# Turning the hidden activations of an FFN with TensorE through PSUM instead of VectorE blocks and block moves by DMA

## The chip, the cores and the metric

The kernel is one launch on one core of a Trainium2 chip. The metric is the device time of that launch in microseconds. Three runs of the kernel before are given, and one execution of it was recorded by the hardware profiler. Engines are called by the names of the profile: PE (TensorE matmuls), PEld (TensorE weight loads), DVE (VectorE), ACT (ScalarE), POOL (GpSimd) and SP (SyncE, which only issues loads here). A name with q behind it (SPq, POOLq) is the engine's queue that issues DMAs.

## What is computed

Two transformer blocks over x of 256 rows by 2048 columns, in float32. The first block has two layers, each with a mixer and a SwiGLU feed-forward; the second has two layers of mixers alone. What the change touches is the feed-forward of the first block:

```python
D_MODEL, SEQ, D_FF = 2048, 256, 5632
def _swiglu(u, w_gu, w_down):
    gate, up = jnp.split(u @ w_gu, 2, axis=-1)
    return (jax.nn.silu(gate) * up) @ w_down
```

u is the normed x. The result is normed again and added to x. Float32 accuracy is wanted from the whole.

## The kernel before

**Stages.** The kernel has six stages, numbered 0 to 5: mixer, FFN, mixer, FFN, mixer, mixer. Stages 1 and 3 are the two FFNs. Each stage multiplies by an input weight (the steps called col) and then by an output weight (the steps called row).

**Float32 by three products.** Each float32 operand is split into a high part (rounded to the fp32r type) and a low part (operand minus high part), and each product is made of three matmuls of 128x512: high times high, high times low, low times high (lines 1117 to 1119 in col, 1164 to 1166 in row). A weight slot is 128x1024 values, 512 KB, loaded by SP into one of four RAW buffers; ACT copies it to WH (line 1645), DVE subtracts to get WL (line 2184). Both are the step prep. A slot feeds 12 matmuls: 2 row tiles t of 128 rows, 2 halves j (or n), 3 products. There are three pairs WH, WL, and prep of slot s+3 can begin when the matmuls of slot s are done. In the order written out by hand, prep of a slot stands two slots ahead of its matmuls.

**An FFN stage.** The 11 chunks q of the 5632 hidden columns are 512 wide. For each q there is a col chunk of the gate (8 slots) and one of the up weight (8 slots). The results for t = 0 and t = 1 lie in two PSUM banks each, from banks 0 to 3. Step gate (ACT, line 1763) writes silu of the gate to the buffer G[q % 2][t] in SBUF, step mul (DVE, line 2267) multiplies it by the up result in place. So G[q % 2] holds a tile of 256 rows by 512 hidden columns with rows on the partitions. The output product needs hidden columns on the partitions, so the tile has to be turned. The row steps take the turned tiles HTH (high) and HTL (low), one k of 128 hidden columns at a time. All 44 k with the first half of the output columns come first (the function left), then 44 with the second half.

**How the tile is turned before.** Four steps, written into the order by the generator hidden, once per q (22 times in all):

- hx on DVE (line 2278): two instructions, each 128x512, that turn 32x32 blocks in place of their positions into the buffer TURNED.
- hx on POOL (line 2870): 16 DMAs of 32 KB each that move the blocks from their partitions to the right ones, into MOVED, which is the same memory as G.
- ht on ACT (line 1769): one copy of 128x1024 to HTH.
- hl on DVE (line 2284): one subtraction of 128x1024 to HTL.

In the order, hx of q stands behind the first slot of the next chunk, and ht and hl stand eight and nine slots later. The row step of k waits for hl of k // 4. The gate of q waits for hl of q - 2.

**PSUM and the order.** The banks 4 to 7 are a ring for short-lived results during the columns of a stage. Nothing of stages 1 and 3 uses it between the start of the columns and the second half of the rows. At the end of the stage before, the step uth (PE line 1092) makes groups of four 128x128 float32 transposes of x into such a bank with ident, the identity matrix in MK, as the other operand. In stage 0, the steps cv_tap (line 1208), cv_out (line 1218) and ot (line 1186 in stages 0, 2, 4 and 5) make the same kind of groups between the weight matmuls. Each engine runs its own instructions in the order of the one list; waits are on semaphores.

Of the kernel before, what the change touches and what calls it, by code (L numbers as in the profile page):

```python
# [121 lines left out]
class Banks:  # L122
# [10 lines left out]
    def take(self, pool, *name):  # L133
        b = min(pool, key=lambda i: self.turn[i])
        self.stamp += 1
        self.turn[b] = self.stamp
        self.before[name], self.now[b], self.where[name] = self.now[b], name, b
        return self.aps[b]
# [70 lines left out]
class Order:  # L209
# [6 lines left out]
    def put(self, *step):  # L216
        self.steps.append(step)
        self.done[step] = self.slot
# [22 lines left out]
def pause(n):  # L241
    for _ in range(n):
        yield
# [7 lines left out]
def write_order(slots):  # L251
# [182 lines left out]
    def ffn(st):  # L434
        def sink(c, t):
            if c % 2 == 0:
                put("gate", st, c, t)
            else:
                put("mul", st, c, t)

        def main():
            yield from cols(st, sink)
            yield from left(st)

        def hidden():
            for q in range(11):
                yield from need(("mul", st, 2 * q + 1, 1))
                yield
                put("hx", st, q)
                yield from pause(8)  # L450
                put("ht", st, q)
                yield
                put("hl", st, q)

        put("gb", st)
        together(main(), hidden())
        right(st)
        cross(st)
# [324 lines left out]
def build(nc, A, out):  # L783
    with ExitStack() as ctx:
# [9 lines left out]
        def steps(name, line=None, by=1):  # L794
            all_steps.append(Steps(ctx.enter_context(nc.semaphore(name)), line or Line(), by))
            return all_steps[-1]
# [10 lines left out]
        GB = WORK[:, 8704:10752]  # L807
        room = [work_at + 4096 * i for i in range(8)] + [big_at + 4 * a for a in (5184, 6400, 7424, 15360)]
        WHL += [(over(f"XH{i}", SLOT, room[2 * i]), over(f"XL{i}", SLOT, room[2 * i + 1])) for i in range(NX)]
        wc_at = -(-nc.sbuf_base // 32) * 32  # L810
        WC = sb("WC", 9 * 128, F32R)[:]
        MK = sb("MK", 8 * 128)[:]
        ONE = sb("ONE", 128)[:]
# [24 lines left out]
        HTL = [over("HTL0", 8192, work_at).rearrange("p (k n) -> p k n", k=32),  # L838
               over("HTL1", 3072, big_at + 4 * 11264).rearrange("p (k n) -> p k n", k=12)]
        G = [[BIG[:, 14336 + 1024 * x + 512 * t:14336 + 1024 * x + 512 * t + 512] for t in range(2)] for x in range(2)]  # L840
        G5 = [[g.rearrange("p (k b n) -> p b k n", k=4, b=4) for g in G[x]] for x in range(2)]
        TURNED = nc.alloc_sbuf_tensor_at("TURNED", [128, 1024], dtype=F32, offset=wc_at)[:]
        MOVED = [BIG[:, a:a + 1024] for a in (14336, 15360)]

        def by_blocks(x):
            return x.rearrange("p k (a n) -> p a k n", n=32)

        Z = v3(BIG, 2)
        ZR = v3(over("ZR", 2 * CHUNKS_EVEN, big_at), 2)
# [159 lines left out]
        def slot_of(s):  # L1009
# [3 lines left out]
            if wd < 64:  # L1013
# [2 lines left out]
            return (v3(x[:, 0:n], kk) for x in (RAW[s % NRAW], wh, wl))  # L1016

        pe, act, dve, pool = Line(), Line(), Line(), Line()
        p_mm, p_ut, p_gd, p_cv, p_hg, p_ns, p_b2 = (
            steps("s_pe_" + n, pe) for n in ("weights", "operand", "gdn", "conv", "hgrn", "nsa", "block2"))  # L1020
        a_hi, a_ut, a_ff, a_z, a_nm, a_gd, a_cv, a_hg, a_og, a_ns, a_b2 = (
            steps("s_act_" + n, act) for n in ("weights", "operand", "ffn", "sink", "norm", "gdn", "conv", "hgrn",
                                               "gate", "nsa", "block2"))
# [4 lines left out]
            steps("s_pool_" + n, pool) for n in ("norm", "nsa", "block2", "root"))  # L1028
        d_raw = [steps(f"s_dma_raw{i}", by=16) for i in range(NRAW)]
        d_x = [steps(f"s_dma_x{i}", by=16) for i in range(4)]  # L1030
        d_first, d_gain, d_const, d_gb, d_ntab, d_w1, d_tab2, d_turn, d_out = (
            steps("s_dma_" + n, by=16) for n in ("first", "norms", "const", "gain", "nsa_tables", "w1", "tables2",
                                                 "turned", "out"))

        def room_of(s):

# [21 lines left out]
        def tensor(e):  # L1058
# [88 lines left out]
            @step  # L1147
            def row(st, k, hf, s, ts, ns):
                raw, wh, wl = slot_of(s)
                xh, xl = (HTH[:, k], HTL[k // 32][:, k % 32]) if st in (1, 3) else (UTH[:, k], UTL[:, k])  # L1150
                on.wait_ge(*v_lo.of(s))
                if st in (1, 3):
                    on.wait_ge(*v_ff.of("hl", st, k // 4))
                else:
                    on.wait_ge(*v_ut.of("ot", st, k if st > 2 else k - k % 2))
                for t in ts:
                    for n in ns:
                        if k == (0 if hf else LEFT[st][0]):
                            banks.take([row_bank(st, t, 2 * hf + n)], "row", st, t, 2 * hf + n)
                            on.wait_ge(*banks.free("row", st, t, 2 * hf + n))  # L1160
                        o = banks.ap("row", st, t, 2 * hf + n)
                        cs = slice(512 * n, 512 * n + 512)
                        lh, ll = xh[:, 128 * t:128 * t + 128], xl[:, 128 * t:128 * t + 128]
                        e.matmul(o, lh, wh[:, 0, cs], start=k == (0 if hf else LEFT[st][0]), stop=False)  # L1164
                        e.matmul(o, lh, wl[:, 0, cs], start=False, stop=False)  # L1165
                        x = e.matmul(o, ll, wh[:, 0, cs], start=False, stop=k == (KTILES[st] - 1 if hf else LEFT[st][-1]))  # L1166
                x.then_inc(*(p_mm.inc("t0", s) if 1 not in ts else p_mm.inc("n0", s) if 1 not in ns else p_mm.inc(s)))

            @step
            def ot(st, k):  # L1170
                b = take("ot", st, k)
                for t in range(2):
                    if st == 0:
                        on.wait_ge(*v_og.of("o", k // 8, k % 8 // 4, t))
                    elif st == 2:
                        on.wait_ge(*v_ns.of("pv", k // 4, t, 2))
                    elif st == 4:
                        on.wait_ge(*v_b2.of("y", st, k // 2, t))
                    else:
                        on.wait_ge(*(v_b2.of("st_o", 3) if k else v_b2.of("yg")))  # L1180
                for j in range(2):
                    if st > 2:
                        b = b if j == 0 else take("ot", st, k + 1)
                    for t in range(2):
                        c = 128 * t if st > 2 else 256 * j + 128 * t
                        x = e.transpose(b[:, c:c + 128], operand_of(st, k + j, t), ident)
                    if j or st > 2:
                        x.then_inc(*p_ut.inc("ot", st, k + j if st > 2 else k))

            @step  # L1190
            def gates1():
# [438 lines left out]
        def scalar(e):  # L1630
# [125 lines left out]
            @step  # L1756
            def gate(st, c, t):
                q = c // 2
                on.wait_ge(*p_mm.of(col_end[st, c]))
                on.wait_ge(*g_rs.of("r", "pre", st))  # L1760
                if q >= 2:
                    on.wait_ge(*v_ff.of("hl", st, q - 2))
                e.activation(G[q % 2][t], banks.ap("acc", st, c, t), ACTF.Silu,
                             scale=HR[:, t:t + 1]).then_inc(*banks.empty(a_ff, "acc", st, c, t))

            @step
            def ht(st, q):
                on.wait_ge(*d_turn.of(st, q, 15))
                e.activation(by_blocks(HTH[:, 4 * q:4 * q + 4]), MOVED[q % 2].rearrange("p (a k n) -> p a k n", a=8, k=4),
                             ACTF.Copy).then_inc(*a_ff.inc("ht", st, q))  # L1770

            @step
            def stat(st, t, part):
# [399 lines left out]
        def vector(e):  # L2173
# [95 lines left out]
                v_ff.also("mul", st, q, t)  # L2269

            @step
            def hx(st, q):
                out = TURNED.rearrange("p (t b k n) -> p t b k n", t=2, b=4, k=4)
                if q or st == 3:
                    on.wait_ge(*d_turn.of(*((st, q - 1) if q else (1, 10)), 15))
                for t in range(2):
                    on.wait_ge(*v_ff.of("mul", st, q, t))
                    e.transpose(out[:, t], G5[q % 2][t]).then_inc(*v_ff.inc("hx", st, q, t))  # L2278

            @step  # L2280
            def hl(st, q):
                on.wait_ge(*a_ff.of("ht", st, q))
                hi, lo = HTH[:, 4 * q:4 * q + 4], HTL[q // 8][:, 4 * q % 32:4 * q % 32 + 4]
                e.tensor_tensor(by_blocks(lo), MOVED[q % 2].rearrange("p (a k n) -> p a k n", a=8, k=4),
                                by_blocks(hi.bitcast(F32)), ALU.subtract).then_inc(*v_ff.inc("hl", st, q))

            @step
            def root(st, t):
# [494 lines left out]
        def gpsimd(e):  # L2783
# [76 lines left out]
                                    ALU.add).then_inc(*g_ns.inc("blk", part, j))  # L2860

            @step
            def hx(st, q):
                src = TURNED.rearrange("p (t b n) -> p t b n", t=2, b=4)
                dst = MOVED[q % 2].rearrange("p (t a n) -> p t a n", t=2, a=4)
                for t in range(2):
                    on.wait_ge(*v_ff.of("hx", st, q, t))
                for a in range(4):
                    for b in range(4):
                        e.dma_start(dst[32 * b:32 * b + 32, :, a], src[32 * a:32 * a + 32, :, b]).then_inc(  # L2870
                            *d_turn.inc(st, q, 4 * a + b))

            @step
            def tables_2():
                stream_made(4)
                for dst, name in ((RT, "c_r32"), (RT16, "c_r16"), (LC, "c_lc"), (CA, "c_ca"), (LTT, "c_lt")):
# [121 lines left out]
```

## Time and profile before

| | |
|---|---|
| median of 3 runs | 2771.85 us (2770.7 to 2773.2) |
| profiled execution, its own time | 2770.7 us |
| its span, first to last instruction | 2768.9 us |
| PE busy | 2741.7 us (99%) |
| DVE busy | 1588.5 us (57%) |
| ACT busy | 1376.8 us (50%) |
| POOL busy | 248.8 us (9%) |
| moved by DMA | 492.67 MB, mean 178 GB/s |

The profiled execution took 1.8 us more than its span and 1.15 us less than the median. A busy time says how long an engine had an instruction in it, not that it could not have been fed faster: matmuls overlap, each is shown with its whole passage through the engine, and their ends are modelled. So for PE the distance from one start to the next is what counts.

### The profile page before, as it was taken

Reading aid. Unit: us, or ns where it says so; the run is one execution under the profiler, and the core shown is the slowest. Engines: PE = TensorE matmul, PEld = TensorE weight load, DVE = VectorE, ACT = ScalarE, POOL = GpSimd, SP = SyncE. Lnnn points to the kernel's source line nnn. Section 1 sums busy time; section 2 is a strip of 40 time slices with the busy share of each in tenths; the row PEclk is TensorE's granted clock in tenths of the full one; section 3 lists DMA queues with packets and bytes.
Section 4 is the critical chain, followed back from the end, with each engine's and each line's share of the span. In section 5 each row is a group of like instructions: output and inputs, shape, how many; then the busy total and the mean of one; then the engine's idle time right before and its main releaser. Section 6 shows DMA issues by size and latency. Waiting matters only on the chain.

```text
span 2768.9 us, 33142 instructions
## 1 busy us (share of the span) xinstructions
PE 2741.7 (99%) x13296; PEld 2284.7 (83%) x13296; DVE 1588.5 (57%) x2214; ACT 1376.8 (50%) x2033; POOL 248.8 (9%) x437
## 2 busy tenths in 40 slices
PE   9999999999999999999999999999999999999998
PEld 7788888888888888888788888888888888887877
DVE  5665777665555555444645555655555554466666
ACT  6655465555444444434644554644444443355565
POOL 0000000001122121100100000021212210000002
PEclk9999999999999999999999999999999999999999
DMA  7865544766677676665665434676767765564444
GB/s 237 136 134 136 108 110 103 175 207 190 201 209 207 203 208 202 201 194 191 213 185 148 137 107 152 192 211 201 209 200 209 207 204 193 195 207 162 160 140 134
DMA packets 224762, 492.67 MB, mean 178 GB/s; under 512 B 21216, under 2 KB 21984, under 8 KB 223968
## 3 DMA queue, kind: packets, MB, share of 16 engines
q1 hardware_dynamic: 210848, 467.78, 58.3%
q0 software_dynamic: 13616, 22.72, 2.4%
q8 instruction: 104, 1.70, 0.3%
q14 instruction: 50, 0.41, 0.0%
q10 hardware_dynamic: 144, 0.05, 0.0%
HBM read 476.84 MB, written 2.10 MB: 173 GB/s over the span
## 4 chain that ended last, share of the span: by engine, by line
PE 89%; DVE 5%; ACT 3%; DMA 1%; issue 1%; POOL 0%; SPq 0%; ACTq 0%; POOLq 0%
PE PS L1117 19%; PE PS L1119 19%; PE PS L1118 19%; PE PS L1164 8%; PE PS L1166 8%; PE PS L1165 8%; DVE WL L2184 2%; DVE WORK L2351 1%; ACT WH L1645 1%; PE PS L1375 1%; PE PS L1503 1%; PE PS L1272 1%; PE PS L1291 1%; PE PS L1092 1%; DVE XL L2184 1%
## 5 line engine op out<-in xcount | busy, mean ns | idle before, releaser
L2184 DVE TENSOR_TENSOR WL<-RAW,WH 128x1024 fp32r<-128x1024 f32 x826 | 1011.1, 1225 | 963.3 <-ACT WH L1645 957.4
L1645 ACT ACTIVATE WH<-RAW 128x1024 fp32r<-128x1024 f32 x830 | 875.4, 1056 | 869.7 <-PE PS L1119 558.5
L1117 PE MATMUL PS<-WH,UTH 128*128 128x512 f32 x2396 | 952.4, 397 | 7.3 <-DVE WL L2184 6.0
L1119 PE MATMUL PS<-WH,UTL 128*128 128x512 f32 x2396 | 935.0, 390 | 0.0
L1118 PE MATMUL PS<-WL,UTH 128*128 128x512 f32 x2396 | 934.2, 390 | 0.0
L1117 PEld LDWEIGHTS PS<-WH,UTH 128*128 128x128 f32 x2396 | 450.4, 188 | 104.7 <-DVE WL L2184 7.0
L1119 PEld LDWEIGHTS PS<-WH,UTL 128*128 128x128 f32 x2396 | 450.1, 188 | 96.5
L1118 PEld LDWEIGHTS PS<-WL,UTH 128*128 128x128 f32 x2396 | 450.7, 188 | 88.1
L1164 PE MATMUL PS<-WH,HTH 128*128 128x512 f32 x656 | 255.2, 389 | 0.0
L1165 PE MATMUL PS<-WL,HTH 128*128 128x512 f32 x656 | 255.2, 389 | 0.0
L1166 PE MATMUL PS<-WH,HTL 128*128 128x512 f32 x656 | 255.2, 389 | 0.0
L2870 POOL DMA_DIRECT2D BIG<-TURNED x352 | 186.1, 538 | 749.5 <-DVE TURNED L2278 672.1
L2792 POOL TENSOR_TENSOR SM<-SM 128x1 f32<-128x1 f32 (+2 forms) x25 | 27.5, 1098 | 1379.0 <-DVE SM L2188 1379.0
L1165 PEld LDWEIGHTS PS<-WL,HTH 128*128 128x128 f32 x656 | 123.1, 188 | 25.7
L1164 PEld LDWEIGHTS PS<-WH,HTH 128*128 128x128 f32 x656 | 123.1, 188 | 25.6
L1166 PEld LDWEIGHTS PS<-WH,HTL 128*128 128x128 f32 x656 | 123.1, 188 | 25.5
L1164 PE MATMUL PS<-WH,UTH 128*128 128x512 f32 x256 | 102.2, 399 | 1.4 <-DVE UTL L2232 1.4
L1166 PE MATMUL PS<-WH,UTL 128*128 128x512 f32 x256 | 99.9, 390 | 0.0
L1165 PE MATMUL PS<-WL,UTH 128*128 128x512 f32 x256 | 99.7, 390 | 0.0
L2184 DVE TENSOR_TENSOR XL<-RAW,XH 128x1024 fp32r<-128x1024 f32 x53 | 63.9, 1220 | 13.1 <-ACT XH L1645 13.0
L1676 ACT ACTIVATE UTH<-PS,GP 128x128 fp32r<-128x128 f32 x160 | 46.1, 386 | 39.7 <-PE PS L1092 39.7
L1645 ACT ACTIVATE XH<-RAW 128x1024 fp32r<-128x1024 f32 x53 | 55.2, 1066 | 19.2 <-DMA RAW<-in_ffn_w_down 7.7
(427 smaller groups left out, 2350.5 us busy)
## 6 DMA issues: line engine op xcount, KB each, us to landing
RAW<-in_ffn_w_gu SPq DMA_DIRECT2D x352, 512.0 KB, 4.5
RAW<-in_ffn_w_down SPq DMA_DIRECT2D x176, 512.0 KB, 4.6
RAW<-in_ab_w_in SPq DMA_DIRECT2D x128, 512.0 KB, 4.7
RAW<-in_nsa_w_in SPq DMA_DIRECT2D x80, 512.0 KB, 3.6
RAW<-in_w_in SPq DMA_DIRECT2D x64, 512.0 KB, 4.1
RAW<-in_ab_w_out SPq DMA_DIRECT2D x32, 512.0 KB, 3.6
RAW<-in_nsa_w_out SPq DMA_DIRECT2D x32, 512.0 KB, 3.9
BIG<-TURNED POOLq DMA_DIRECT2D x352, 32.0 KB, 3.4
```

What stands on the lines that cost most here:

```text
L1092: x = e.transpose(b[:, 128 * j:128 * j + 128], H[:, t, 128 * (4 * q + j):128 * (4 * q + j) + 128], ident)
L1117: e.matmul(o, lh, wh[:, j], start=k + j == 0, stop=False)
L1118: e.matmul(o, lh, wl[:, j], start=False, stop=False)
L1119: x = e.matmul(o, ll, wh[:, j], start=False, stop=k + j == NKT - 1)
L1164: e.matmul(o, lh, wh[:, 0, cs], start=k == (0 if hf else LEFT[st][0]), stop=False)
L1165: e.matmul(o, lh, wl[:, 0, cs], start=False, stop=False)
L1166: x = e.matmul(o, ll, wh[:, 0, cs], start=False, stop=k == (KTILES[st] - 1 if hf else LEFT[st][-1]))
L1272: x = e.matmul(b[:, 128 * h:128 * h + 128], LT[:, h], XX[:, h, 0], start=True, stop=True)
L1645: e.activation(wh, raw, ACTF.Copy).then_inc(*a_hi.inc(s))
L1676: e.activation(UTH[:, kk, 128 * t:128 * t + 128], b[:, 128 * j:128 * j + 128], ACTF.Copy, scale=GP[:, st, kk:kk + 1]).then_inc(*a_ut.inc(" ...
L2184: e.tensor_tensor(wl, raw, wh.bitcast(F32), ALU.subtract).then_inc(*v_lo.inc(s))
L2870: e.dma_start(dst[32 * b:32 * b + 32, :, a], src[32 * a:32 * a + 32, :, b]).then_inc(*d_turn.inc(st, q, 4 * a + b))
```

## The change

The turn is done by TensorE. For each q and each t a new PE step ht makes four 128x128 transposes of G[q % 2][t] into one bank of the ring 4 to 7. ACT copies that bank (128x512) to HTH, DVE subtracts to get HTL. The DVE block turns, the 16 DMAs of POOL and the buffers TURNED and MOVED are gone. In the order, ht of t = 0 stands behind the first slot of the next chunk and ht of t = 1 behind the second; for the last q both stand behind the first slot of the rows. The row step waits for the low part of t = 1, the gate of q for the transposes of q - 2.

```diff
@@ order, ffn(st).hidden @@
             for q in range(11):
                 yield from need(("mul", st, 2 * q + 1, 1))
                 yield
-                put("hx", st, q)
-                yield from pause(8)
-                put("ht", st, q)
-                yield
-                put("hl", st, q)
+                for t in range(2):
+                    put("ht", st, q, t)
+                    if q < 10:
+                        yield
@@ tensor, row @@
-                    on.wait_ge(*v_ff.of("hl", st, k // 4))
+                    on.wait_ge(*v_ff.of("ht", st, k // 4, 1))
@@ tensor @@
+            def ht(st, q, t):
+                g = G[q % 2][t]
+                b = take("ht", st, q, t)
+                on.wait_ge(*v_ff.of("mul", st, q, t))
+                for j in range(4):
+                    x = e.transpose(b[:, 128 * j:128 * j + 128], g[:, 128 * j:128 * j + 128], ident)
+                x.then_inc(*p_ht.inc(st, q, t))
@@ scalar, gate @@
-                    on.wait_ge(*v_ff.of("hl", st, q - 2))
+                    on.wait_ge(*p_ht.of(st, q - 2, t))
@@ scalar @@
-            def ht(st, q):
-                on.wait_ge(*d_turn.of(st, q, 15))
-                e.activation(by_blocks(HTH[:, 4 * q:4 * q + 4]), MOVED[q % 2].rearrange("p (a k n) -> p a k n", a=8, k=4),
-                             ACTF.Copy).then_inc(*a_ff.inc("ht", st, q))
+            def ht(st, q, t):
+                on.wait_ge(*p_ht.of(st, q, t))
+                e.activation(HTH[:, 4 * q:4 * q + 4, 128 * t:128 * t + 128], v3(banks.ap("ht", st, q, t), 4),
+                             ACTF.Copy).then_inc(*a_ff.inc("ht", st, q, t))
@@ vector @@
-            def hx(st, q):
-                ...
-            def hl(st, q):
-                ...
+            def ht(st, q, t):
+                lo = HTL[q // 8][:, 4 * q % 32:4 * q % 32 + 4, 128 * t:128 * t + 128]
+                on.wait_ge(*a_ff.of("ht", st, q, t))
+                e.tensor_tensor(lo, v3(banks.ap("ht", st, q, t), 4),
+                                HTH[:, 4 * q:4 * q + 4, 128 * t:128 * t + 128].bitcast(F32),
+                                ALU.subtract).then_inc(*banks.empty(v_ff, "ht", st, q, t))
@@ gpsimd @@
-            def hx(st, q):
-                ...
-                for a in range(4):
-                    for b in range(4):
-                        e.dma_start(dst[32 * b:32 * b + 32, :, a], src[32 * a:32 * a + 32, :, b]).then_inc(
-                            *d_turn.inc(st, q, 4 * a + b))
```

## Rows read from the trace of the kernel before

**Rows 1.** The page, shares of the engines and 40 slices

```profile
PE 2741.7 (99%) x13296; PEld 2284.7 (83%) x13296; DVE 1588.5 (57%) x2214; ACT 1376.8 (50%) x2033; POOL 248.8 (9%) x437
PEclk9999999999999999999999999999999999999999
```

**Rows 2.** Busy time by stretch: the two FFN stages, then one with four transpose groups

```profile
640.00:1320.00 680.00, 680.00 (x3003) 562.99 (x3003) 350.31 (x318) 293.66 (x307) 93.80 (x178) 1.00 0.67 202
1790.00:2468.00 678.00, 678.00 (x2993) 561.41 (x2992) 349.76 (x311) 291.21 (x293) 94.81 (x178) 1.00 0.67 203
...
616.00:624.00 8.00, 8.00 (x44) 6.64 (x43) 7.15 (x15) 5.99 (x16) 0.00 (x0) 1.00 0.62 175
```

**Rows 3.** Instructions of single lines: ns shortest/median/longest, first and last start

```profile
L2278 DVE STREAM_TRANSPOSE TURNED<-BIG x44: 669/688/707, 671.8 to 2249.4; 128x512 f32<-128x512 f32 x44
L2870 POOL DMA_DIRECT2D BIG<-TURNED x352: 533/539/575, 673.8 to 2258.7; - x176
L1769 ACT ACTIVATE HTH<-BIG x22: 1043/1057/1057, 693.2 to 2269.1; 128x1024 fp32r<-128x1024 f32 x22
L2284 DVE TENSOR_TENSOR HTL<-BIG,HTH x22: 1216/1218/1221, 696.4 to 2273.1; 128x1024 fp32r<-128x1024 f32 x22
L1688 ACT ACTIVATE UTH<-PS x8: 592/596/610, 1646.2 to 1705.4; 128x512 fp32r<-128x512 f32 x8
L2242 DVE TENSOR_TENSOR UTL<-PS,UTH x8: 680/686/692, 1646.8 to 1706.1; 128x512 fp32r<-128x512 f32 x8
L1092 PE MATMUL PS<-MK,H x160: 270/272/273, 617.4 to 2641.4; 128*128 128x128 f32 x160
```

**Rows 4.** Timeline of PE: start us, us, line; two transpose groups twelve matmuls apart

```profile
53.20 0.39 PE L1119 MATMUL PS<-WH,UTL 128*128 128x512 f32 x1
53.44 0.60 PE L1218 MATMUL PS<-MK,WORK 128*128 128x128 f32 x4
53.79 0.49 PE L1117 MATMUL PS<-WH,UTH 128*128 128x512 f32 x1
54.11 0.39 PE L1118 MATMUL PS<-WL,UTH 128*128 128x512 f32 x1
54.34 0.39 PE L1119 MATMUL PS<-WH,UTL 128*128 128x512 f32 x1
...
56.42 0.39 PE L1119 MATMUL PS<-WH,UTL 128*128 128x512 f32 x1
56.66 0.60 PE L1218 MATMUL PS<-MK,WORK 128*128 128x128 f32 x4
```

**Rows 5.** Timeline of PE, stage 1: 36 starts during DMAs of POOL, 57 without

```profile
673.91 0.39 PE L1117 MATMUL PS<-WH,UTH 128*128 128x512 f32 x1
...
682.07 0.39 PE L1117 MATMUL PS<-WH,UTH 128*128 128x512 f32 x1
...
1090.75 0.39 PE L1117 MATMUL PS<-WH,UTH 128*128 128x512 f32 x1
...
1103.67 0.39 PE L1117 MATMUL PS<-WH,UTH 128*128 128x512 f32 x1
```

**Rows 6.** Timeline of DVE, ACT, PE and POOL around the end of the first chunk pair

```profile
668.92 0.39 PE L1119 MATMUL PS<-WH,UTL 128*128 128x512 f32 x1
669.35 1.41 DVE L2267 SCALAR_TENSOR_TENSOR BIG<-PS,SM,BIG 128x512 f32<-128x512 f32 x2 [0.34 <-PE PS L1119]
670.68 1.22 DVE L2184 TENSOR_TENSOR WL<-RAW,WH 128x1024 fp32r<-128x1024 f32 x1
671.87 0.39 PE L1117 MATMUL PS<-WH,UTH 128*128 128x512 f32 x1
672.13 1.06 ACT L1645 ACTIVATE WH<-RAW 128x1024 fp32r<-128x1024 f32 x1 [1.66 <-PE PS L1119]
673.23 1.23 DVE L2184 TENSOR_TENSOR WL<-RAW,WH 128x1024 fp32r<-128x1024 f32 x1
673.80 8.47 POOL L2870 DMA_DIRECT2D BIG<-TURNED  x16 [24.27 <-DVE TURNED L2278]
```

**Rows 7.** Timeline of PE, stage 5: a group whose result the next matmul needs

```profile
2602.53 0.39 PE L1166 MATMUL PS<-WH,UTL 128*128 128x512 f32 x1
2602.76 0.60 PE L1186 MATMUL PS<-MK,BIG 128*128 128x128 f32 x4
2604.07 0.50 PE L1164 MATMUL PS<-WH,UTH 128*128 128x512 f32 x1 [0.71 <-DVE UTL L2232]
...
2604.64 0.39 PE L1166 MATMUL PS<-WH,UTL 128*128 128x512 f32 x1
```

More of the change, by code:

```diff
@@ L809, in build @@
         WHL += [(over(f"XH{i}", SLOT, room[2 * i]), over(f"XL{i}", SLOT, room[2 * i + 1])) for i in range(NX)]
-        wc_at = -(-nc.sbuf_base // 32) * 32
         WC = sb("WC", 9 * 128, F32R)[:]
@@ L840, in build @@
         G = [[BIG[:, 14336 + 1024 * x + 512 * t:14336 + 1024 * x + 512 * t + 512] for t in range(2)] for x in range(2)]
[L841 to L846, printed above, removed]
         Z = v3(BIG, 2)
@@ L1018, in build @@
         pe, act, dve, pool = Line(), Line(), Line(), Line()
-        p_mm, p_ut, p_gd, p_cv, p_hg, p_ns, p_b2 = (
-            steps("s_pe_" + n, pe) for n in ("weights", "operand", "gdn", "conv", "hgrn", "nsa", "block2"))
+        p_mm, p_ut, p_ht, p_gd, p_cv, p_hg, p_ns, p_b2 = (
+            steps("s_pe_" + n, pe) for n in ("weights", "operand", "hidden", "gdn", "conv", "hgrn", "nsa", "block2"))
         a_hi, a_ut, a_ff, a_z, a_nm, a_gd, a_cv, a_hg, a_og, a_ns, a_b2 = (
@@ L1030, in build @@
         d_x = [steps(f"s_dma_x{i}", by=16) for i in range(4)]
-        d_first, d_gain, d_const, d_gb, d_ntab, d_w1, d_tab2, d_turn, d_out = (
-            steps("s_dma_" + n, by=16) for n in ("first", "norms", "const", "gain", "nsa_tables", "w1", "tables2",
-                                                 "turned", "out"))
+        d_first, d_gain, d_const, d_gb, d_ntab, d_w1, d_tab2, d_out = (
+            steps("s_dma_" + n, by=16) for n in ("first", "norms", "const", "gain", "nsa_tables", "w1", "tables2", "out"))
         def room_of(s):
@@ L1188, in ot @@
                         x.then_inc(*p_ut.inc("ot", st, k + j if st > 2 else k))
+            @step
+            def ht(st, q, t):
[5 more added lines that the diff above has]
+                x.then_inc(*p_ht.inc(st, q, t))
             @step
@@ L2271, in hx @@
             @step
-            def hx(st, q):
[L2273 to L2280, printed above, removed]
-            def hl(st, q):
[L2282 to L2285, printed above, removed]
+            def ht(st, q, t):
[4 more added lines that the diff above has]
+                                ALU.subtract).then_inc(*banks.empty(v_ff, "ht", st, q, t))
             @step
@@ L2862, in hx @@
             @step
-            def hx(st, q):
[L2864 to L2867, printed above, removed]
-                for a in range(4):
-                    for b in range(4):
-                        e.dma_start(dst[32 * b:32 * b + 32, :, a], src[32 * a:32 * a + 32, :, b]).then_inc(
-                            *d_turn.inc(st, q, 4 * a + b))
-            @step
             def tables_2():
```

## The prediction

> **What bounds the kernel now.** I read the page first. PE is busy 99% of the span and its granted clock stands in the top tenth in all 40 slices; DVE has 57%, ACT 50%, POOL 9% [rows 1]. That is an average, so I asked for the two FFN stages alone. From 640 to 1320 us PE is busy 680.00 of 680.00 us, from 1790 to 2468 us 678.00 of 678.00, both at clock 1.00 (the 2.4 GHz level), while DVE and ACT work about half of either stretch [rows 2]. The reader is to see that in the stages the change touches PE never sits idle. But a matmul is shown with 0.39 us although the next one starts sooner, so "busy" would hide slack in the feeding. The timeline decides: 36 starts from 673.91 to 682.07 us are 8.16 us, or 0.2267 us each; 57 starts from 1090.75 to 1103.67 are 12.92 us, again 0.2267 [rows 5]. PE runs the stages in lockstep, one 128x512 matmul every 0.2267 us, and nothing else shows in this rhythm. So a thing taken from DVE, ACT, POOL or the DMA queues brings nothing there, and a thing put into PE's queue costs its full distance between starts, once for each time it is done. As the instructions of PE are strictly one behind another through all six stages, what is lost in stages 1 and 3 is not won back later.
>
> **What is removed.** Per q: two block turns on DVE, 2 x 0.688 = 1.38 us; the subtraction, 1.22 us; the copy on ACT, 1.06 us; 16 DMAs issued by POOL, 16 x 0.539 = 8.6 us of POOL [rows 3]. Over 22 q that is 57 us of DVE, 23 of ACT and 190 of POOL. I count all of it as 0 us of time: it lies beside PE's matmuls, and PE waits for none of it in the stretches of [rows 2]. The moves are 352 x 32 KB = 11.5 MB; a lighter load on the DMA engines could only help if PE waited for weights, and it doesn't there.
>
> **What is added off PE.** Per q two copies of 128x512 out of PSUM on ACT and two such subtractions on DVE. The same forms stand in stage 2: 0.596 and 0.686 us [rows 3]. So ACT has 1.19 us per q in place of 1.06, DVE 1.37 in place of 2.60. Cost 0 us, hidden behind the twelve matmuls of a slot (12 x 0.2267 = 2.72 us), if prep of the weights stays in time. Behind the waiting copy on ACT stands prep of slot s+4, and PE waits for that. Take s as the last slot of a chunk pair, with its last matmul at 668.92 [rows 6]. Today prep of s+3 ends on DVE at 670.68 + 1.22 = 671.90, and slot s+3 begins at 669.15 + 2 x 2.72 = 674.59 (669.15 is 668.92 + 0.23): 2.7 us in hand. After the change the group of t = 0 comes behind slot s+1, at 671.87. Its four transposes end near 672.47, the copy ends near 673.2, prep of s+4 on ACT near 674.3, on DVE near 675.5. Slot s+4 begins at 674.59 + 2.72 plus about 1.0 for the two groups, 678.3. Again about 2.8 us in hand: the lateness of prep and the lateness of its user nearly cancel. If that cover were gone, the copies and subtractions would stand in PE's way, at most 44 x (0.596 + 0.686) = 56 us.
>
> **The new wait on PE.** Each group waits for its mul. In [rows 6] the two mul run from 669.35 to 670.76, the first ends near 670.1, and PE gets to its group at 671.87: 1.7 us early; the second group, a slot later, has 4 us. For the last q both groups stand 2.72 us behind the last column matmul, with the second mul done after about 1.8 (668.92 to 670.76): 0.9 us in hand. The bank of the ring was emptied long before, since nothing else uses banks 4 to 7 here. The gate's wait falls earlier than before, not later. The low part of a chunk is needed by rows that are far behind, even for the last q (its first k is the 41st row slot). Cost 0.
>
> **What is added on PE.** 2 stages x 11 q x 2 t = 44 groups of four, 176 transposes, all in the queue that sets the end. The same thing (four 128x128 float32 transposes between fp32r matmuls of 128x512, wait fulfilled) stands in the trace many times. In [rows 4], from the matmul before the group at 53.20 to the third behind it at 54.34 are 1.14 us, of which three matmul distances are 0.68: 0.46 us. That isn't all: the matmuls behind a group start 0.23 us apart, not 0.2267, for a while. From 53.20 to 56.42 there are twelve matmuls and one group: 3.22 - 2.72 = 0.50 us. At other such places the twelve-matmul reading gives 0.48 to 0.51, so I take 0.50, since ten of eleven pairs of groups here stand just twelve matmuls apart, as those of [rows 4]. The two groups of the last q stand side by side; the second then costs only the 0.45 of its own distance. Sum: 40 x 0.50 + 2 x 0.95 = 21.9 us. Bounds: 44 x 0.45 = 19.8 and 44 x 0.51 = 22.4.
>
> **Sum.** Against the profiled execution: span 2768.9 + 21.9 = 2790.8, with the 1.8 us around it 2792.6. The median lies 1.15 above that execution, so the median after comes to 2771.85 + 21.9 = 2793.7 us, 0.8% slower. What a measurement of this kernel can tell from no change is about 0.2%, 5.5 us; the sum is four times that.
>
> **A price that reads otherwise.** The row of the transposes gives 272 ns for one [rows 3], and someone who goes by it gets 176 x 0.272 = 47.9 us, or 2820. I don't take it: four in a row are shown as 0.60 us, so (0.60 - 0.272) / 3 = 0.11 us lies between two starts [rows 4]; 272 ns is the passage of one through the array, which the neighbours overlap. The Trainium skill (TensorE: Matmul & The Clock Gate, "Part 4: PE-mode transpose") states about 275 ns for a transpose in a kernel's context and 390 ns alone. By that rule the trace agrees on the duration, and taken as a cost it would give an estimate near 2820 us.
>
> **The rivals.**
>
> 1. *Each transpose costs its shown duration.* 2820 us. For it: nothing but the row of 272 ns. Against it: no group of the trace with its wait fulfilled costs over 0.51 us. Chance 0.03.
> 2. *A group waits, or makes prep late.* Its place is the first group of each q (mul not done) or slot s+4 (weights not ready). The margins are 1.7 us, 0.9 us in the last q, and 2.8 us, and it decides from there on. A group whose result the next matmul needs costs 2.11 - 0.68 = 1.43 us [rows 7], which is 0.93 more than a plain one; if all 44 were so, 2793.7 + 41 = 2835 us, if only the first of each q, 2814. A fall of the granted clock belongs here: four groups within 8 us leave it at 1.00 [rows 2], so I give that almost nothing. Chance of the whole rival 0.05.
> 3. *The transposes slip in free.* Then the time stays within 5.5 us of 2771.85, and a group must cost under 0.125 us. For it: weight loads overlap matmuls. Against it: none read costs under 0.45. It holds also the case that about 16 us come back from something I don't see. Chance 0.03.
> 4. *The moves slow the matmuls today, and their end pays for more than the transposes.* This is the one with the other sign: the FFN stages have 2 x (22 x 8 + 88) x 12 = 6336 matmuls; to get 5.5 us below 2771.85 they must gain 27.4 us, 4.3 ns of 226.7 each, giving 2766 us. Against it: the distance is 0.2267 us during the DMAs of POOL and without them [rows 5]. Chance 0.02. The Trainium skill (VectorE: DVE Perf Modes, "Rules for kernel authors") says to transpose 128x128 on TensorE where PSUM will do as the destination; as a rule for the time it would put the result on this side, and these rows don't bear it out in a kernel that PE bounds.
>
> **How the numbers follow.** The forecast has 0.87; all of it is slower by over 0.2%, with rivals 1 and 2 that makes 0.95 for slower, 0.03 for the same, 0.02 for faster. The bounds of the group's price give 2791.7 to 2794.3; the three runs lie 1.2 below and 1.4 above their median. With a little room for a few exposed waits the range is 2790 to 2797; it leaves out about 2 in 10, the rivals and the rim of the forecast.
>
> **What would show each step.** Right: in the page after, a new PE group of 128x128 with PS<-MK,BIG x176 at a line of its own; stages 1 and 3 each about 11 us longer, PE busy throughout; 3.22 us from the matmul before a group to the twelfth behind it; POOL down by about 190 us; DVE busy down by about 27 us and ACT up by about 3; no idle time ahead of the new group, and prep done over 2 us before its slot. Wrong: PE idle before the new group with DVE's mul as releaser, or before line-1117 matmuls with DVE's WL; a matmul distance other than 0.2267 us far from the groups; a clock under 1.00 in either stage.

## The result, and the profile after

The changed kernel takes 2792.58 us (median of 4 runs, 2790.19 to 2793.2). The kernel before, in the runs beside it, takes 2772.52. The ratio is 1.007 with a 95% interval of 1.0058 to 1.0083: 20.1 us slower. The profiled execution of the changed kernel has a span of 2790.9 us, 22.0 over the span of before.

The page after, its shares of the engines (compare [rows 1]):

```profile
PE 2763.0 (99%) x13472; PEld 2302.3 (82%) x13472; DVE 1566.4 (56%) x2192; ACT 1379.0 (49%) x2055; POOL 62.9 (2%) x85
```

PE has 176 instructions more, POOL has lost 186 us and DVE 22. The 186 us of POOL and the moves are gone from the profile, and the time went the other way.

The two FFN stages after, busy time by stretch (columns as in [rows 2]: stretch, its length, busy time and number of instructions of PE, PEld, DVE, ACT and POOL, granted clock, DMA share, GB/s):

```profile
640.00:1320.00 680.00, 680.00 (x3045) 562.74 (x3044) 331.68 (x299) 289.96 (x311) 1.23 (x2) 1.00 0.59 190
1801.00:2479.00 678.00, 678.00 (x3033) 561.15 (x3032) 331.17 (x293) 286.64 (x296) 1.23 (x2) 1.00 0.60 192
```

PE is as full as before and the clock stays at 1.00. What changed is what PE is full of. The timeline of PE after, stage 1, from the last matmul of a chunk pair over both groups of its q (answers to [rows 4]):

```profile
670.40 0.39 PE L1110 MATMUL PS<-WH,UTL 128*128 128x512 f32 x1
...
673.12 0.40 PE L1110 MATMUL PS<-WH,UTL 128*128 128x512 f32 x1
673.36 0.60 PE L1187 MATMUL PS<-MK,BIG 128*128 128x128 f32 x4
673.71 0.49 PE L1108 MATMUL PS<-WH,UTH 128*128 128x512 f32 x1
674.03 0.39 PE L1109 MATMUL PS<-WL,UTH 128*128 128x512 f32 x1
674.27 0.39 PE L1110 MATMUL PS<-WH,UTL 128*128 128x512 f32 x1
...
676.35 0.39 PE L1110 MATMUL PS<-WH,UTL 128*128 128x512 f32 x1
676.58 0.60 PE L1187 MATMUL PS<-MK,BIG 128*128 128x128 f32 x4
...
1115.07 0.39 PE L1108 MATMUL PS<-WH,UTH 128*128 128x512 f32 x1
...
1118.24 0.39 PE L1157 MATMUL PS<-WH,HTL 128*128 128x512 f32 x1
1118.47 1.03 PE L1187 MATMUL PS<-MK,BIG 128*128 128x128 f32 x8
1119.26 0.48 PE L1155 MATMUL PS<-WH,HTH 128*128 128x512 f32 x1
...
1136.81 0.39 PE L1157 MATMUL PS<-WH,HTL 128*128 128x512 f32 x1
```

From 673.12 to 676.35 there are twelve matmuls and one group: 3.23 - 2.72 = 0.51 us. To see what all groups cost, follow one and the same matmul through both traces. The last of the first chunk pair starts at 668.92 before [rows 6] and at 670.40 after, 1.48 later, ahead of any group. The one at 1103.67 before [rows 5] starts at 1115.07 after, 11.40 later. Between them lie 20 groups: 9.92 / 20 = 0.496 us each. The timeline of PE before has the partner of the last line:

```profile
1124.52 0.39 PE L1166 MATMUL PS<-WH,HTL 128*128 128x512 f32 x1
```

There the lag is 12.29: the eight transposes of the last q, side by side, cost 0.89. So stage 1 loses 9.92 + 0.89 = 10.81 us, and stage 3, read in the same way, again 10.81. That is 21.6 of the 22.0 us of span.

The new instructions by line, after (columns as in [rows 3]; under the groups stands who waits):

```profile
L1187 PE MATMUL PS<-MK,BIG x176: 270/272/273, 673.4 to 2270.9; 128*128 128x128 f32 x176
L1769 ACT ACTIVATE HTH<-PS x44: 595/599/600, 674.0 to 2271.2; 128x512 fp32r<-128x512 f32 x44
L2275 DVE TENSOR_TENSOR HTL<-PS,HTH x44: 678/691/694, 674.6 to 2272.0; 128x512 fp32r<-128x512 f32 x44
```

No line under the first of them names anything that PE waited for. The copy and the subtraction take 599 and 691 ns, as their likes in [rows 3].

### The profile page after: what moved, and what is told of

It reads as the page before. It is cut to its first block, busy times and chain, and to the rows that moved or that the text cites. A ratio compares the mean times of both kernels' runs of the same rounds, so it can differ in the third digit from the quotient of the medians.

```text
span 2790.9 us, 33039 instructions
## 1 busy us (share of the span) xinstructions
PE 2763.0 (99%) x13472; PEld 2302.3 (82%) x13472; DVE 1566.4 (56%) x2192; ACT 1379.0 (49%) x2055; POOL 62.9 (2%) x85
## 4 chain that ended last, share of the span: by engine, by line
PE 89%; DVE 5%; ACT 3%; DMA 2%; issue 1%; POOL 0%; SPq 0%; ACTq 0%; POOLq 0%
PE PS L1108 19%; PE PS L1110 19%; PE PS L1109 19%; PE PS L1155 8%; PE PS L1157 8%; PE PS L1156 8%; DVE WL L2184 2%; DVE WORK L2343 1%; ACT WH L1645 1%; PE PS L1375 1%; PE PS L1503 1%; PE PS L1272 1%; PE PS L1187 1%; PE PS L1291 1%; PE PS L1083 1%
## 5 line engine op out<-in xcount | busy, mean ns | idle before, releaser
L1769 ACT ACTIVATE HTH<-PS 128x512 fp32r<-128x512 f32 x44 | 26.1, 599 | 78.2 <-PE PS L1187 78.2
```

## The experiments

Seven kernels ran, in two sets, each beside runs of the kernel before. In the first set, with a median of 2771.03 us for before, ran the changed kernel once more, the groups beside the old path, both groups side by side, and one by one. In the second, with 2770.6, ran the change without its transposes, twice the groups, and the groups ahead of their data. The lag of a kernel is read as above, as the start of one and the same matmul in its trace minus that in the trace of before.

**The changed kernel once more.**

> The changed kernel as it is, once more, beside the runs below. Theory (44 groups of four transposes in PE's queue, each 0.49 to 0.50 us, the last pair 0.89, nothing else): 21.6 us above before, so near 2793, span about 2791. Rival (the difference is mostly chance between executions of a program): the difference to before would wander by several us from the first measurement's 20.1.

2792.9 us (5 runs, 2791.67 to 2793.23), span 2791.1, ratio 1.0076 (1.0064 to 1.0089). The lag over stage 1 is again 10.81 us and over stage 3 again 10.81. The difference isn't chance.

**Groups beside the old path.** The kernel before with transposes of x that nobody reads:

```diff
                 put("hx", st, q)
-                yield from pause(8)
+                put("hd", st, q, 0)
+                if q < 10:
+                    yield
+                put("hd", st, q, 1)
+                yield from pause(7 if q < 10 else 8)
@@ tensor @@
+            def hd(st, q, t):
+                b = take("hd", st, q, t)
+                for j in range(4):
+                    e.transpose(b[:, 128 * j:128 * j + 128], H[:, t, 128 * j:128 * j + 128], ident)
```

> The kernel before with all of its DVE turns, POOL moves, copies and subtractions, and beside them 44 groups of four 128x128 float32 transposes of x into unused banks, at the places in PE's queue where the change puts its own; nobody reads them. Theory (what the change takes from DVE, POOL and the DMA queues is worth nothing, the groups are all): 21.6 us over before, the time of the changed kernel, near 2793. Rival (the moves cost something today, which the change saves, and the transposes cost that much more than shown): above the changed kernel by that saving, 2795 to 2800.

2793.59 us (4 runs, 2790.76 to 2794.48), ratio 1.0078 (1.0063 to 1.0094), span 2791.4. Its page:

```profile
PE 2763.2 (99%) x13472; PEld 2302.6 (82%) x13472; DVE 1588.5 (57%) x2214; ACT 1376.7 (49%) x2033; POOL 249.3 (9%) x437
```

DVE, ACT and POOL work as much as in [rows 1], PE as much as after the change, and the time is that of the change. By the lag, stages 1 and 3 lose 10.75 us each, against 10.81 after the change. The 186 us of POOL, the 22 us of DVE and 11.5 MB of moves that the change saves are worth nothing that can be measured.

**The change without its transposes.** ACT and DVE read the unturned tile in SBUF (the copy waits for mul in place of the transposes, and the output product is left wrong); the cut shows the copy, and the subtraction is edited likewise:

```diff
-                for j in range(4):
-                    x = e.transpose(b[:, 128 * j:128 * j + 128], g[:, 128 * j:128 * j + 128], ident)
...
-                e.activation(HTH[:, 4 * q:4 * q + 4, 128 * t:128 * t + 128], v3(banks.ap("ht", st, q, t), 4),
+                e.activation(HTH[:, 4 * q:4 * q + 4, 128 * t:128 * t + 128], v3(G[q % 2][t], 4),
```

> The changed kernel without the transposes: ACT copies and DVE subtracts straight from the unturned tile in SBUF, in the same places, so the hidden activations are left unturned and the output product is of the wrong layout; all else is as in the changed kernel. Theory (PE's queue is all): the time of before, 2772 to 2773, although DVE, POOL and DMA are relieved. Rival (the relief is worth something and the transposes cost more than 21.6 us): below before by over 2 us, 2765 to 2770. Rival (the added copies and subtractions cost something): above before, 2775 or more.

2770.93 us (10 runs, 2769.65 to 2772.99) against 2770.6, ratio 1.0 (0.9991 to 1.0009), span 2769.2. Its page:

```profile
PE 2743.0 (99%) x13296; PEld 2286.3 (83%) x13296; DVE 1562.9 (56%) x2192; ACT 1381.1 (50%) x2055; POOL 63.2 (2%) x85
```

Here the relief of POOL and DVE is there and the transposes are not, and the time is that of before. The lag moves by 0.02 us at most over either FFN stage. The two kernels close the question from both sides: the transposes alone are the 21 us.

**Twice the groups.** The changed kernel and, four slots after its own groups, two of x into unused banks (hd as above):

```diff
+                if q == 10:
+                    yield
+                yield from pause(2)
+                for t in range(2):
+                    put("hd", st, q, t)
+                    yield
```

> The changed kernel with 44 more groups of four transposes, of x, into unused banks, at the fifth and sixth slots of the chunk after, each twelve matmuls or more from any other group. Theory (each group adds 0.49 to 0.50 us of PE's queue): 21.8 us above the changed kernel, near 2814. Rival (part of the first 44 was a one-off price such as a wait or a code effect, not a price per group): the second 44 add clearly less or more than the first, under 19 or over 25 us.

2812.76 us (4 runs, 2812.34 to 2814.11), ratio 1.0151 (1.0136 to 1.0166), span 2811.1. That is 19.9 over the changed kernel run in the other set and 20.0 by the spans, short of the 21.8 expected and not far above the 19 at which the rival begins. The lags decide against that rival: over stage 1 the kernel loses 21.78 us, over stage 3 21.79, so 43.6 in all and 22.0 for the second 44 groups (none of which stand side by side). The missing 2 us lie outside the FFN stages, where executions of one kernel differ too (last section).

**Both groups of a q side by side.**

```diff
                 yield
-                for t in range(2):
-                    put("ht", st, q, t)
-                    if q < 10:
-                        yield
+                put("ht", st, q, 0)
+                put("ht", st, q, 1)
```

> Both groups of a q stand side by side behind the first slot of the next chunk, as in the last q, so PE makes eight transposes in a row; 22 pairs in all. Theory (a transpose costs 0.11 us, and each return from transposes to fp32r matmuls costs about 0.05 us more, once per return): a pair costs 0.89 instead of 0.99 us, 20 x 0.10 = 2.0 us less than the changed kernel, near 2790.6, span about 2789. Rival (the cost is per transpose alone, 0.124 each however they stand): no difference, 2792.6. Second rival (the second bank of a pair waits for the second mul): slower than the changed kernel, with PE idle ahead of the transposes.

2789.97 us (5 runs, 2787.59 to 2791.81), span 2787.9. That is 2.9 us less than the changed kernel beside it by the medians, but the runs of the two touch. The timeline of PE is what decides:

```profile
671.76 0.40 PE L1108 MATMUL PS<-WH,UTL 128*128 128x512 f32 x1
672.00 1.04 PE L1185 MATMUL PS<-MK,BIG 128*128 128x128 f32 x8
672.79 0.48 PE L1106 MATMUL PS<-WH,UTH 128*128 128x512 f32 x1
673.11 0.40 PE L1107 MATMUL PS<-WL,UTH 128*128 128x512 f32 x1
673.34 0.39 PE L1108 MATMUL PS<-WH,UTL 128*128 128x512 f32 x1
673.57 0.39 PE L1106 MATMUL PS<-WH,UTH 128*128 128x512 f32 x1
673.80 0.39 PE L1107 MATMUL PS<-WL,UTH 128*128 128x512 f32 x1
674.02 0.39 PE L1108 MATMUL PS<-WH,UTL 128*128 128x512 f32 x1
```

From 671.76 to 673.34 are three matmuls and eight transposes, 1.58 - 0.68 = 0.90 us, and from 671.76 to 674.02 six matmuls, 2.26 - 1.36 = 0.90 again: behind eight, the matmuls are back in the 0.2267 rhythm almost at once. All 22 pairs read 0.88 to 0.90. The stages lose 9.83 us each, 1.96 in sum less than after the change, as the theory had it.

**One by one.** Each transpose behind another slot (the step hp makes one transpose of a group of four); ht on ACT and DVE behind the fourth:

```diff
                 for t in range(2):
-                    put("ht", st, q, t)
-                    if q < 10:
-                        yield
+                    for j in range(4):
+                        put("hp", st, q, t, j)
+                        if j == 3:
+                            put("ht", st, q, t)
+                        if (t, j) != (1, 3):
+                            yield
```

> The 176 transposes stand one by one, each behind another slot of twelve matmuls, so that there are 176 returns to the matmuls instead of 42. Theory (0.11 each plus about 0.05 per return): 176 x 0.16 = 28.2 us over before, near 2800, 6.6 above the changed kernel. Rival A (0.124 each, whatever stands around): 2794, as the changed kernel. Rival B (a single transpose slips under the weight load and passage of its neighbours and costs only the time of its 128 columns): 176 x 0.057 = 10 us over before, near 2782; 0.057 is a quarter of the distance of a matmul of 512 columns.

2795.54 us (4 runs, 2794.83 to 2796.01), span 2794.0, ratio 1.0087 (1.0073 to 1.0101). None of the three was right: it is 2.6 over the changed kernel, not 6.6, not 0, and not 11 below. The timeline of PE:

```profile
674.26 0.39 PE L1113 MATMUL PS<-WH,UTL 128*128 128x512 f32 x1
674.49 0.27 PE L1191 MATMUL PS<-MK,BIG 128*128 128x128 f32 x1
674.52 0.47 PE L1111 MATMUL PS<-WH,UTH 128*128 128x512 f32 x1
674.83 0.39 PE L1112 MATMUL PS<-WL,UTH 128*128 128x512 f32 x1
675.06 0.40 PE L1113 MATMUL PS<-WH,UTL 128*128 128x512 f32 x1
...
677.14 0.39 PE L1113 MATMUL PS<-WH,UTL 128*128 128x512 f32 x1
677.37 0.27 PE L1191 MATMUL PS<-MK,BIG 128*128 128x128 f32 x1
```

At the third matmul behind, a single costs 0.80 - 0.68 = 0.12; at the twelfth 2.88 - 2.72 = 0.16. Read over all 176 it is 0.12 to 0.17, mean 0.144: about half of them keep the 0.12 and the other half pick up 0.03 to 0.05 more. So it is 0.144 us each when alone, 0.124 in fours, 0.112 in eights. The part "0.05 per return, each time" of the theory is refuted.

**The groups ahead of their data.**

```diff
                 yield from need(("mul", st, 2 * q + 1, 1))
-                yield
-                for t in range(2):
-                    put("ht", st, q, t)
-                    if q < 10:
-                        yield
+                put("ht", st, q, 0)
+                put("ht", st, q, 1)
```

> Both groups of a q stand right behind the last slot of its chunk, ahead of the next slot, so PE comes to them before mul is done. It takes the margin away that the prediction counted as 1.7 us. Theory (the rhythm of the rows of before: the last matmul starts at 668.92, mul of t = 0 ends near 670.1, of t = 1 at 670.76): PE idles about 1.0 us before the first group and about 0.3 before the second, and resumes about 1.2 us later per q than in the changed kernel, 22 x 1.2 = 26 us, near 2819. Rival (mul or the semaphores are later than shown): 2825 or more. Rival (PE's order lets the next matmuls go ahead of the waiting transposes): no more than the changed kernel, 2793.

2817.7 us (4 runs, 2817.14 to 2819.93), span 2816.0, ratio 1.017 (1.0153 to 1.0187): 24.8 over the changed kernel of the other set, 26 expected. The timeline around the end of the first chunk pair:

```profile
669.24 0.39 PE L1107 MATMUL PS<-WH,UTL 128*128 128x512 f32 x1
669.67 1.41 DVE L2264 SCALAR_TENSOR_TENSOR BIG<-PS,SM,BIG 128x512 f32<-128x512 f32 x2 [0.34 <-PE PS L1107]
670.47 1.31 PE L1184 MATMUL PS<-MK,BIG 128*128 128x128 f32 x8 [0.84 <-DVE BIG L2264]
671.16 1.26 ACT L1766 ACTIVATE HTH<-PS 128x512 fp32r<-128x512 f32 x2 [3.10 <-PE PS L1184]
671.54 0.48 PE L1105 MATMUL PS<-WH,UTH 128*128 128x512 f32 x1
```

This is how the wait looks when it is there: PE sits idle 0.84 us with mul as its releaser, 22 times (18.6 us in the view of the waits), and the next matmul starts 2.30 us behind the last one of the chunk. Without the wait the transposes could have started at 669.47, a matmul's distance behind; they start 1.0 us later, at 670.47. The wait for the second mul lies inside the eight, which take 1.31 us in place of 1.04 (both groups side by side, above). These are the 1.0 and 0.3 us that were expected. Such a pair costs 2.17 to 2.22 us in place of 0.99. Nothing behind the waiting transposes went ahead of them.

## Why the prediction was right

2793.7 was forecast, 2792.6 measured; by spans 2790.8 against 2790.9. That the spans agree to 0.1 us is partly luck. The two stages cost 21.6 us, not 21.9. The rest of the 22.0 between the two executions arises outside these stages: a lag of 1.48 us was there ahead of the first group, and 1.1 of it went away again, 0.95 in stage 2 and 0.15 behind stage 3 (last section).

- **PE in lockstep, all else free.** Shown by the kernel without transposes (2770.93) and by the one with the old path and transposes (2793.59). The weight of the argument lay on [rows 2] and [rows 5], and both held.
- **The price of a group.** 0.50 us was taken out of [rows 4]; 0.496 is measured over 20 groups. The pair of the last q was put at 0.95 and cost 0.89: the second group was counted at its full 0.45, and the drag behind the first, which two groups side by side don't show, was still counted. That is 0.1 us too much in the sum of 21.9; the 40 groups of the others were counted 0.2 too high.
- **The copies and subtractions.** No cost, as said. The margin of prep is shown by the timeline of DVE and PE after:

```profile
670.83 1.41 DVE L2267 SCALAR_TENSOR_TENSOR BIG<-PS,SM,BIG 128x512 f32<-128x512 f32 x2 [0.34 <-PE PS L1110]
...
675.57 1.23 DVE L2184 TENSOR_TENSOR WL<-RAW,WH 128x1024 fp32r<-128x1024 f32 x1 [0.26 <-ACT WH L1645]
679.56 0.39 PE L1110 MATMUL PS<-WH,UTL 128*128 128x512 f32 x1
679.79 0.39 PE L1108 MATMUL PS<-WH,UTH 128*128 128x512 f32 x1
```

  WL of slot s+4 is done at 676.80 and its matmuls begin at 679.79: 3.0 us in hand, where 2.8 were worked out.
- **The new wait.** The mul that the first group needs was ahead of it: it starts at 670.83, its group at 673.36. PE shows no idle time at line 1187. That the margin was real, and what it would have cost without it, the kernel with the groups ahead of their data shows: 1.2 us per q. In the last q, where 0.9 us was said to be in hand, DVE shows the two mul of stage 1 as

```profile
1115.95 1.41 DVE L2267 SCALAR_TENSOR_TENSOR BIG<-PS,SM,BIG 128x512 f32<-128x512 f32 x2 [0.34 <-PE PS L1110]
```

  They end at 1117.36, and the eight transposes start at 1118.47: 1.1 us in hand.
- **The busy times.** POOL down 186 us (190 said), ACT up 2.2 (3 said), DVE down 22 (27 said). The DVE figure was summed from single durations, and neighbours on an engine overlap in the record: the two turns of a q stand in the timeline of before as 1.30 us together, not 2 x 0.688 (1.7 us over 22 q), and one that follows or precedes a subtraction of the weights overlaps it by about 0.1 us as well, which makes up most of the rest.
- **The rivals.** The one at 2820 us (272 ns for each) fell: 272 ns is what the changed kernel's row says, and 0.11 to 0.14 us is what it costs. The Trainium skill (TensorE: Matmul & The Clock Gate, "Part 4: PE-mode transpose") has about 275 ns in a kernel's context (its example is bf16, here it is float32); as a duration the trace agrees, as a price it would be twice too high. The one with the other sign fell with the two kernels of the first point. The Trainium skill (VectorE: DVE Perf Modes, "Rules for kernel authors") says to turn 128x128 on TensorE where PSUM will do; here DVE turns blocks and DMAs move them at no cost in time, and TensorE costs 20 us, since it is the engine that has none to spare.

The medians differ by 20.1 us in the first measurement and 21.9 in the second, against 21.6 in the two stages; the last section shows where executions scatter.

## What to carry to other kernels

In a stage where one engine never idles, price an edit by what it adds to that engine's queue, read as distance between starts with a dozen instructions behind it, and count relief of the others as nothing until a wait is shown. The duration in an instruction's row is a passage, not a price: here 272 ns against 0.11 to 0.14 us. And a longer way over idle engines and DMA queues can be the cheap one, as long as its result is due late: here eight slots, 22 us, lay between the turn and the copy.

## What the runs showed of the hardware

**The rhythm behind a transpose.** Behind a group of four the fp32r matmuls start 0.23 us apart for about nine of them and then fall back to 0.2267; behind eight they are back after about three; behind single ones about half show the drag and half don't. The readers of the result don't make it: behind the groups that nobody reads, beside the old path, the drag is the same (0.45 to 0.46 us at the third matmul behind, 0.49 to 0.50 at the twelfth). What makes it is open; it is worth 2 us here.

**A fall of the clock that comes and goes.** In stage 2, with a wait for WL that both kernels have, PE idles and goes on. The timeline of PE before, and then the row of the stretch behind it in the view of busy time by stretch (the granted clock is the third number from the end):

```profile
1385.61 0.50 PE L1117 MATMUL PS<-WH,UTH 128*128 128x512 f32 x1 [2.92 <-DVE WL L2184]
...
1387.46 0.63 PE L1117 MATMUL PS<-WH,UTH 128*128 128x512 f32 x1
1387.88 0.63 PE L1118 MATMUL PS<-WL,UTH 128*128 128x512 f32 x1
```

```profile
1386.60:1390.00 3.40, 3.40 (x9) 2.30 (x7) 1.21 (x2) 0.00 (x0) 0.00 (x0) 0.51 0.68 171
```

The same two views after the change:

```profile
1398.21 0.50 PE L1108 MATMUL PS<-WH,UTH 128*128 128x512 f32 x1 [2.62 <-DVE WL L2184]
...
1399.24 0.39 PE L1109 MATMUL PS<-WL,UTH 128*128 128x512 f32 x1
```

```profile
1398.40:1400.90 2.50, 2.50 (x12) 1.98 (x11) 2.02 (x2) 0.00 (x0) 0.00 (x0) 1.00 0.46 113
```

With the clock at the lower level (1.2 GHz) the starts are 0.42 us apart in place of 0.23, and the lag between the traces shrinks from 12.60 to 11.05 us there. In the nine executions profiled it fell five times, behind 2.68 to 3.03 us of idle time, and stayed four times, behind 2.22 to 2.79. The changed kernel has one of each (it fell behind 3.03 and stayed behind 2.62), so the change doesn't decide it; it is worth 1.5 us. Two other places scatter between executions. Over the first 20 us of the kernel the two executions of the changed kernel come apart by 0.7 us, and at the end of stage 0, where PE waits for weights by a varying amount, by 0.4 more (ahead of the first group the lag is 1.48 us in the one and 0.35 in the other). These three places are as large as what the medians scatter about the 21.6 us of the two stages; that they make all of it isn't shown, since only one execution of each measurement has a trace.
